# A layer's modulation columns moved from VectorE to ScalarE, and rotary work spread over the units of a weight stream

## The chip, the cores and the metric

One core of a Trainium2 chip. The metric is the device time of one execution in microseconds, median of several runs. Engines are named TensorE (PE in the profile; its weight loads are PEld), VectorE (DVE), ScalarE (ACT), GpSimd (POOL) and the DMA queue of the sync engine (SP).

## What is computed

Two blocks on 256 tokens of width 1024, all in float32. The first block has two layers: a retention layer and a forgetting-attention layer, each modulated by a conditioning vector `c`. The second block is a layer of windowed attention beside a gated recurrence, and a feed-forward network. The part that matters here is the entry of the first layer:

```
shift, scale, gate = jnp.split(c_act @ mod_w[i] + mod_b[i], 3, axis=-1)
h = _rms_norm(x, norm_g[i]) * (1.0 + scale[:, None, :]) + shift[:, None, :]
q, k, v, g = jnp.split(h @ w_in, [RET_DK, 2 * RET_DK, 2 * RET_DK + RET_DV], axis=-1)
q = _rope(q..., positions) * (RET_HK ** -0.5)
k = _rope(k..., positions)
```

`_rope` multiplies halves of each head of 256 by the cosine and sine of position times frequency; the positions are data, so the angles are made in the kernel: a product, a reduction to one turn in several steps, and Sin on ScalarE.

## The kernel before, in words

**Weights as a stream of units.** TensorE multiplies float32 as three products of rounded parts: `whi*ahi + wlo*ahi + whi*alo` (lines 382 to 384, and 493 to 495 in `rows_unit`). All weights pass through one list, `items`. An item "w" is a unit: 128 partitions x 1024 weights (two k-tiles of 512 columns, or one of 1024), 512 KB. SP loads it into one of eight tiles `raw`, ScalarE rounds it to `whi` (line 1796 records all its copies), VectorE subtracts to get `wlo` (line 1057 records all its two-tensor operations), and TensorE uses it for 12 matmuls. There are three buffers of `whi` and `wlo`, so ScalarE makes unit u when TensorE is done with unit u - 3. An item "mod" is a row block of the second layer's modulation weights, or of a gate's: VectorE alone adds it to `acc` (scalar_tensor_tensor, line 1066), in its place in the list. On VectorE and ScalarE `ring_to(u)` does all items up to unit u. Around the change the list reads: mod, 12, mod, 13, mod, 14, mod, 15, mod, 16, 17, 18, mod, 19, 20, 21, mod, 22, 23, 24, 25, mod, 26, 27, 28, mod, 29, 30.

**First layer's h.** Units 0 to 11 are used as the k-tiles of h come. For k-tile k, TensorE sums `c_act @ mod_w` for shift and scale into one column of PSUM each (`own_rows`, line 444, and `other_rows`, line 449, which reads a partial sum `macc` made by VectorE in `mod_sums`) and increments the semaphore `sums`. `modulated(k)` on VectorE makes two columns of `AB` from them: shift plus bias, and (scale + 1 + bias) times the norm's gain, and increments `mod0`. `x0_high(k)` on ScalarE waits for `mod0`, applies the two columns to the transposed normed x (Identity with scale and bias), and rounds to `ahi`; `x0_low(k)` on VectorE makes `alo`. SP waits for `mod0` too, before it loads the fourth and the fifth group of modulation weights (`load_mod`). `mbc` and `mb1` hold bias columns, `g_col` the gains.

**Rotary stage.** Units 12 to 27 are four column chunks of four units: q, q, k, k. A chunk c fills two banks of PSUM, `G[2*(c%2)+m]` for the token halves m = 0, 1. `angles` makes the reduced angles in three parts on VectorE (eleven small operations and a cast), ScalarE takes two Sin of them behind unit 17's `whi`. `rope(n, bank)`, n = 2c + m, is four VectorE operations: two products of 128x512 and two sums of 128x256. TensorE transposes the rope's result (`turn_qk(n)`, line 403): rope 2c - 2 behind the first unit of chunk c, rope 2c - 1 behind the second. Before, VectorE runs all three angle parts ahead of unit 13, and both ropes of a chunk one after the other at the chunk's end. In units 28 to 31 `turn_qk(6)` and `turn_qk(7)` stand behind units 29 and 30, and VectorE's statistics `weighed(0)` behind `ring_to(30)`.

**What sets the order.** Each engine runs its own list, written by hand; VectorE works up to two units ahead of TensorE (`ring_to(u + 2)`). An instruction that waits holds all behind it on its engine. On ScalarE, ahead of unit 14's `whi`, stand the copies of v, a table load and two Silu for the gates. POOL waits for all 32 rope operations before it fills a tile for the second layer's gate.

Of the kernel before, what the change touches and what calls it, by code (L numbers as in the profile page):

```python
# [6 lines left out]
P = 128  # L7
# [10 lines left out]
ALU = mybir.AluOpType  # L18
ACT = mybir.ActivationFunctionType
# [151 lines left out]
def program(nc, x_in, c_in, pos_in, mod_w, mod_b, norm_g, ret_w_in, ret_w_out, fox_w_in, fox_b_f,  # L171
            fox_q_gain, fox_k_gain, fox_w_out, final_g, norm1_w, w_in2, lb_logits, hgrn_nw, w_out2,
            norm2_w, w_gate_up, w_down, final_nw, consts, out):
    with ExitStack() as ctx:
        def sb(name, shape, dt=F32):
            return ctx.enter_context(nc.sbuf_tensor(name, shape, dt))

        sig = Signals(lambda name: ctx.enter_context(nc.semaphore(name)))
# [16 lines left out]
        rows = sb("rows", [P, P])  # L195
        cols = sb("cols", [P, 44])
        mbc = sb("mbc", [P, 16])
        mb1 = sb("mb1", [P, 8])
        cact = sb("cact", [P, 8])
        AB = sb("AB", [P, 2, 16])  # L200
        st = sb("st", [P, 80])
# [16 lines left out]
        G = [ctx.enter_context(nc.psum_tensor(f"G{i}", [P, 512], F32)) for i in range(4)]  # L218
# [10 lines left out]
        g_col = cols[:, 0:16].rearrange("p (a k) -> p a k", a=2)  # L229
# [16 lines left out]
        def sums_of(k, a):  # L246

            return (G[a] if k == 0 else T[a] if k == 1 else T[2 + k % 2])[:, 256 + a:257 + a]
# [801 lines left out]
        def _(e):  # L1050
            on_ = Once(e)

            def bc(ap, *shape):
                return ap.to_broadcast(list(shape))

            def tt(o, a, b, op, name):
                e.tensor_tensor(o, a, b, op).then_inc(sig[name], 1)  # L1057

            def ts(o, a, s1, s2, op0, op1, name):
                if op1 is None:  # L1060
                    e.tensor_scalar(o, a, s1, None, op0).then_inc(sig[name], 1)  # L1061
                else:
                    e.tensor_scalar(o, a, s1, s2, op0, op1).then_inc(sig[name], 1)
# [9 lines left out]
            sums = {}  # L1073
# [24 lines left out]
            def ring_to(u):  # L1098

                while done[0] <= item_of[u]:  # L1100
                    item()
# [24 lines left out]
                    else:  # L1126
                        stt(o, a, col(cact, r), o, ALU.mult, ALU.add, "macc" if last else "mod_sum")

            def modulated(k):

                on_.wait_ge(sig["sums"], k + 1)
                on_.wait_ge(sig["columns"], 3)
                tt(AB[:, 0, 8 + k:9 + k], sums_of(k, 0), mbc[:, k:k + 1], ALU.add, "mod0")
                ts(AB[:, 0, k:k + 1], sums_of(k, 1), mb1[:, k:k + 1], g_col[:, 0, k:k + 1], ALU.add, ALU.mult, "mod0")

            def x0_low(k):
                on_.wait_ge(sig["h_hi"], k + 1)
                tt(alo[:, k, :], stage0[:, k % 4, :], ahi[:, k, :].bitcast(F32), ALU.subtract, "x0")
# [7 lines left out]
            t = T[bank_of["rows"]]  # L1146
            copy(cols[:, 0:44], t[:, 8:52], "columns")
            copy(mbc[:, :], t[:, 54:70], "columns")
            ts(mb1[:, :], t[:, 62:70], 1.0, None, ALU.add, None, "columns")
            modulated(0)  # L1150
            ring_to(0)
            x0_low(0)
            copy(gains[:, 1:2], t[:, 53:54], "rows_read")
            ts(gains[:, 0:1], t[:, 52:53], 0.125, None, ALU.mult, None, "rows_read")
            tt(n1f[:, :], t[:, 70:78], n1_col, ALU.mult, "rows_read")
            mod_sums(1, 0, 4)
            ring_to(1)
            modulated(1)
            ring_to(2)
            x0_low(1)  # L1160
            for g in (2, 3, 4):
                k, u = 2 * g - 2, 3 * g - 3
                mod_sums(g, 0, 4)
                ring_to(u - 1)
                mod_sums(g, 4, 7)
                ring_to(u)
                modulated(k)
                modulated(k + 1)
                x0_low(k)
                ring_to(u + 1)  # L1170
                x0_low(k + 1)
# [19 lines left out]
            def rope(n, src):  # L1191

                m = n % 2
                on_.wait_ge(sig["sincos"], 2)
                on_.wait_ge(sig["rope"], 4 * n)
                A = rot[:, 0, :].rearrange("p (b n) -> p b n", n=P)
                B = rot[:, 1, :].rearrange("p (b n) -> p b n", n=P)
                s = src[:, :].rearrange("p (b n) -> p b n", n=P)
                tt(A, s, bc(cs[:, 0, m, None, :], P, 4, P), ALU.mult, "rope")
                tt(B, s, bc(cs[:, 1, m, None, :], P, 4, P), ALU.mult, "rope")  # L1200
                A4 = rot[:, 0, :].rearrange("p (h t n) -> p h t n", t=2, n=P)
                B4 = rot[:, 1, :].rearrange("p (h t n) -> p h t n", t=2, n=P)
                o = qr[:, n % 2, :].rearrange("p (h t n) -> p h t n", t=2, n=P)
                on_.wait_ge(sig["rope"], 4 * n + 2)
                on_.wait_ge(sig["qk_turned"], n - 1)
                tt(o[:, :, 0, :], A4[:, :, 0, :], B4[:, :, 1, :], ALU.subtract, "rope")
                tt(o[:, :, 1, :], B4[:, :, 0, :], A4[:, :, 1, :], ALU.add, "rope")

            def angles(part):

                BIG, PI = 12582912.0, 3.1415925
                if part == 0:
                    on_.wait_ge(sig["small_in"], 64)
                    copy(posf[:, :], posi[:, :], "posf")
                    on_.wait_ge(sig["small_in"], 64)
                    on_.wait_ge(sig["posf"], 1)
                    for m in range(2):
                        ts(tmp_r[:, m, :], invf, posf[:, m:m + 1], None, ALU.mult, None, "angle")
                    on_.wait_ge(sig["angle"], 2)
                    ts(tmp_k, tmp_r, 1.0 / (2 * np.pi), BIG, ALU.mult, ALU.add, "angle")  # L1220
                    on_.wait_ge(sig["angle"], 3)
                    ts(tmp_k, tmp_k, BIG, None, ALU.subtract, None, "angle")
                elif part == 1:
                    for i, step in enumerate((6.28125, 1014 * 2.0 ** -19, 2 * np.pi - 6.28125 - 1014 * 2.0 ** -19)):
                        on_.wait_ge(sig["angle"], 4 + i)
                        stt(tmp_r, tmp_k, -step, tmp_r, ALU.mult, ALU.add, "angle")
                else:
                    on_.wait_ge(sig["angle"], 7)
                    ts(tmp_k, tmp_r, np.pi / 2, -2 * np.pi, ALU.is_gt, ALU.mult, "angle")
                    on_.wait_ge(sig["angle"], 8)  # L1230
                    stt(tmp_k, tmp_r, np.pi / 2, tmp_k, ALU.add, ALU.add, "angle")
                    on_.wait_ge(sig["angle"], 9)
                    ts(tmp_r, tmp_r, PI, -PI, ALU.min, ALU.max, "angle")
                    ts(tmp_k, tmp_k, PI, -PI, ALU.min, ALU.max, "angle")
# [5 lines left out]

            u = 12
            ring_to(u)
            for part in range(3):
                angles(part)
            for c in range(4):
                for k in range(4):
                    ring_to(u + 2)
                    u += 1
                    if c == 3 and k >= 2:
                        scored(k - 2)  # L1250
                on_.wait_ge(sig["g"], done_at[u - 1, 1])
                for m in range(2):
                    rope(2 * c + m, G[2 * (c % 2) + m])


            def weighed(h):
# [39 lines left out]
            def chunk_of(between):  # L1296
                nonlocal u
                for k in range(4):
                    ring_to(u + 2)
                    u += 1  # L1300
                    for f, *a in between[k]:
                        f(*a)

            chunk_of([[(weighed, 0)], [], [(gated, 0)], [(scored, 2)]])
            chunk_of([[(scored, 3)], [(weighed, 1)], [(left_low, 8)], [(left_low, 10), (gated, 1)]])
            chunk_of([[(weighed, 2)], [(left_low, 12)], [(left_low, 14)], [(gated, 2)]])
            chunk_of([[], [], [(left_low, 16)], [(left_low, 18)]])
# [304 lines left out]
            for k in range(4):  # L1612
# [5 lines left out]
                c, m = k // 2, k % 2  # L1618
# [61 lines left out]
            for m in range(2):  # L1680
                t = T[bank_of["hg_values", m]]
# [107 lines left out]
        def _(e):  # L1789
            on_ = Once(e)  # L1790

            def act(o, a, f, name=None, scale=1.0, bias=0.0, accum=None):
                if accum is not None:
                    d = e.activation(o, a, f, scale=scale, bias=bias, accum_out=accum)
                elif f == ACT.Copy:
                    d = e.activation(o, a, f, scale=scale)  # L1796
                else:
                    d = e.activation(o, a, f, scale=scale, bias=bias)  # L1798
                if name:
                    d.then_inc(sig[name], 1)  # L1800
# [62 lines left out]

            def x0_high(k):

                on_.wait_ge(sig["x0_turned"], k + 1)
                on_.wait_ge(sig["mod0"], 2 * k + 2)
                on_.wait_ge(sig["x0"], k - 3)
                act(stage0[:, k % 4, :], T[2 + k % 2][:, 0:256], ACT.Identity, "h_in", scale=col(AB[:, 0, :], k), bias=col(AB[:, 0, :], 8 + k))
                on_.wait_ge(sig["h_in"], k + 1)  # L1870
                act(ahi[:, k, :], stage0[:, k % 4, :], ACT.Copy, "h_hi")
# [83 lines left out]
            def chunk_of(between):  # L1955
                nonlocal u
                for k in range(4):
                    ring_to(u + 2)
                    u += 1
                    for f, *a in between[k]:  # L1960
                        f(*a)
                on_.wait_ge(sig["g"], done_at[u - 1, 1])
# [187 lines left out]
            for k in range(4):  # L2150
# [3 lines left out]
                c, m = k // 2, k % 2  # L2154
# [255 lines left out]
```

## Time and profile before

| | |
|---|---|
| median of 3 runs | 727.55 us (726.63 to 727.56) |
| profiled execution | 727.51 us, its span 725.7 us |
| TensorE busy | 705.6 us, 97% |
| VectorE busy | 501.6 us, 69% |
| ScalarE busy | 380.0 us, 52% |
| GpSimd busy | 15.9 us, 2% |

Times in the rows are microseconds from the start of the span, and durations of one instruction; instructions of an engine overlap their neighbours by a part of their duration. A bracket at the end of a row is the idle time of the engine ahead of it, and what ended it. Matmul ends are modelled, so starts are the better guide.

### The profile page before, as it was taken

The page shows a single profiled execution, that of the slowest core. Times are in us where ns is not written, and L with a number is a line of the kernel's source. Part 1 is how long each engine was busy: PE and PEld are TensorE (multiplying, and loading weights), DVE is VectorE, ACT ScalarE, POOL GpSimd, SP SyncE. Part 2 cuts the span into 40 slices and gives each one's busy share as a digit, 9 for nine tenths or more (in the row PEclk, how much of TensorE's full clock was granted, in tenths as well). Part 3 has the DMA queues.
Part 4 walks back from the last instruction along what each step waited for, and adds up shares of the span by engine and source line. Part 5 has one row for each costly group of instructions (what it writes and reads, how often), then busy time and mean ns, then how long its engine had stood idle before and what let it go on. Part 6 is the DMA issues. An engine that isn't in the chain of part 4 may idle for free.

```text
span 725.7 us, 9362 instructions
## 1 busy us (share of the span) xinstructions
PE 705.6 (97%) x3534; PEld 577.7 (80%) x3534; DVE 501.6 (69%) x727; ACT 380.0 (52%) x559; POOL 15.9 (2%) x33
## 2 busy tenths in 40 slices
PE   6999999999999999999999899999999999999996
PEld 5887877777887788788887688878888888888884
DVE  4789888787956778665658689955775555555444
ACT  5347544565544565553565654554565445444342
POOL 6000000000000000000000000000000000000000
PEclk8799999999999999999999999999999999999999
DMA  9998865676986357733444553333456655555611
GB/s 295 369 373 312 295 202 182 197 227 210 312 296 205 113 178 249 244 117 115 147 148 143 146 174 117 117 116 117 129 187 206 192 180 180 180 196 178 197 61 58
DMA packets 74476, 138.96 MB, mean 191 GB/s; under 512 B 5748, under 2 KB 18272, under 8 KB 74432
## 3 DMA queue, kind: packets, MB, share of 16 engines
q1 hardware_dynamic: 72816, 134.82, 57.3%
q10 hardware_dynamic: 736, 1.90, 0.7%
q0 software_dynamic: 880, 1.64, 0.6%
q8 instruction: 28, 0.46, 0.3%
q14 instruction: 16, 0.13, 0.1%
HBM read 137.31 MB, written 1.05 MB: 191 GB/s over the span
## 4 chain that ended last, share of the span: by engine, by line
PE 89%; DVE 6%; ACT 2%; issue 2%; DMA 1%; SPq 0%; DVEq 0%; ACTq 0%
PE G L382 23%; PE G L384 23%; PE G L383 22%; PE T L403 5%; PE T L771 2%; DVE wlo L1057 2%; PE T L884 2%; DVE arena L1057 1%; PE T L761 1%; PE G L493 1%; DMA arena<-in_mod_w_dram 1%; PE G L495 1%; PE G L494 1%; PE T L444 1%; ACT whi L1796 1%
## 5 line engine op out<-in xcount | busy, mean ns | idle before, releaser
L1057 DVE TENSOR_TENSOR wlo<-raw,whi 128x1024 fp32r<-128x1024 f32 x202 | 246.1, 1223 | 127.2 <-ACT whi L1796 126.5
L382 PE MATMUL G<-whi,ahi 128*128 128x512 f32 x760 | 307.8, 405 | 4.3 <-DVE wlo L1057 4.3
L384 PE MATMUL G<-whi,alo 128*128 128x512 f32 x760 | 297.0, 391 | 0.0
L383 PE MATMUL G<-wlo,ahi 128*128 128x512 f32 x760 | 296.1, 390 | 0.0
L1796 ACT ACTIVATE whi<-raw 128x1024 fp32r<-128x1024 f32 x202 | 212.9, 1060 | 123.5 <-PE G L384 108.4
L382 PEld LDWEIGHTS G<-whi,ahi 128*128 128x128 f32 x760 | 142.9, 188 | 36.9 <-DVE wlo L1057 8.9
L384 PEld LDWEIGHTS G<-whi,alo 128*128 128x128 f32 x760 | 142.6, 188 | 31.3
L383 PEld LDWEIGHTS G<-wlo,ahi 128*128 128x128 f32 x760 | 143.1, 188 | 28.0 <-issue 1.2
L1798 ACT ACTIVATE arena<-T,st 128x128 f32<-128x128 f32 (+2 forms) x56 | 21.7, 478 | 30.4 <-DVE st L1429 30.4
L1796 ACT ACTIVATE ahi<-T 128x512 fp32r<-128x512 f32 x25 | 15.0, 599 | 41.8 <-PE T L403 41.8
L403 PE MATMUL T<-head,arena 128*128 128x128 f32 x244 | 36.8, 275 | 0.0
L403 PEld LDWEIGHTS T<-head,arena 128*128 128x128 f32 x244 | 29.3, 139 | 9.4 <-issue 2.0
L1798 ACT ACT_TABLE_LOAD x27 | 34.6, 1283 | 2.8 <-issue 1.8
L1066 DVE SCALAR_TENSOR_TENSOR acc<-raw,cact,acc 128x1024 f32<-128x1024 f32 x24 | 30.8, 1282 | 1.1
L1057 DVE TENSOR_TENSOR alo<-T,ahi 128x512 fp32r<-128x512 f32 x25 | 17.3, 691 | 17.7 <-ACT ahi L1796 17.7
L1057 DVE TENSOR_TENSOR arena<-arena 128x512 f32<-128x512 f32 (+7 forms) x46 | 23.0, 551 | 0.8 <-ACT arena L1798 0.5
L1429 DVE TENSOR_REDUCE st<-T 128x2 f32<-128x512 f32 (+1 forms) x18 | 11.6, 686 | 15.5 <-PE T L761 15.5
L1798 ACT ACTIVATE st<-st 128x1 f32<-128x1 f32 (+3 forms) x21 | 4.3, 205 | 26.9 <-DVE st L1061 18.3
L1066 DVE SCALAR_TENSOR_TENSOR arena<-arena,cact 128x512 f32<-128x512 f32 (+1 forms) x24 | 16.4, 685 | 0.8
L884 PEld LDWEIGHTS T<-arena 128*128 128x128 f32 x128 | 15.4, 191 | 0.9 <-DVE arena L1057 0.4
L1796 ACT ACTIVATE arena<-arena 128x512 f32<-128x512 f32 x14 | 8.3, 638 | 14.4 <-DVE arena L1057 14.4
L884 PE MATMUL T<-arena 128*128 128x128 f32 x128 | 15.7, 276 | 0.0
(227 smaller groups left out, 606.8 us busy)
## 6 DMA issues: line engine op xcount, KB each, us to landing
raw<-in_ret_w_in_dram SPq DMA_DIRECT2D x48, 512.0 KB, 5.4
raw<-in_w_gate_up_dram SPq DMA_DIRECT2D x40, 512.0 KB, 3.6
raw<-in_mod_w_dram SPq DMA_DIRECT2D x32, 512.0 KB, 4.8
raw<-in_fox_w_in_dram SPq DMA_DIRECT2D x32, 512.0 KB, 4.8
raw<-in_w_in_dram SPq DMA_DIRECT2D x28, 512.0 KB, 3.5
raw<-in_w_down_dram SPq DMA_DIRECT2D x22, 512.0 KB, 4.3
arena<-in_mod_w_dram SPq DMA_DIRECT2D x16, 512.0 KB, 8.8
raw<-in_ret_w_out_dram SPq DMA_DIRECT2D x16, 512.0 KB, 5.6
```

The lines of the kernel that those rows point to most:

```text
L382: e.matmul(o, ah, wh, start=first and k == 0, stop=False)
L383: e.matmul(o, ah, wl, start=False, stop=False)
L384: done = e.matmul(o, al, wh, start=False, stop=last and k == 1)
L403: d = e.transpose(t[:, n * P:(n + 1) * P], s, idf)
L444: e.matmul(sums_of(SUMMED[g][i], a), mod_tile(g)[:, a, r, i * P:(i + 1) * P], cact[:, r:r + 1], start=r == r0, stop=False)
L771: d = e.matmul(t[:, 65 * a:65 * a + 65], PT[:, g % 2, (a * (m + 1) + j) * P:(a * (m + 1) + j + 1) * P], v[:, j, h, :], start=j == 0, stop= ...
L884: d = e.matmul(t[:, h * P:(h + 1) * P], k[:, h, m * P:(m + 1) * P], q[:, h, m * P:(m + 1) * P], start=True, stop=True)
L1057: e.tensor_tensor(o, a, b, op).then_inc(sig[name], 1)
L1066: e.scalar_tensor_tensor(out=o, in0=a, scalar=s, in1=b, op0=op0, op1=op1).then_inc(sig[name], 1)
L1429: e.tensor_reduce(st[:, 44 + 4 * r:44 + 4 * r + n], t[:, :].rearrange("p (h n) -> p h n", h=n), AX.X, ALU.max, negate=True).then_inc(sig[f ...
L1796: d = e.activation(o, a, f, scale=scale)
L1798: d = e.activation(o, a, f, scale=scale, bias=bias)
```

## The change

It does three things.

1. The first layer's shift and scale columns are made by ScalarE at the head of `x0_high(k)`, as two Identity activations on one column each; `modulated` goes from VectorE. Since (sum + mb1) * g = sum * g + mb1 * g, VectorE makes the product `mb1 * g` for all eight k-tiles once, in a second half of `mb1`.
2. The three parts of `angles` run behind `ring_to(14)`, `ring_to(15)` and `ring_to(16)`, where all three ran behind `ring_to(12)`.
3. Of a chunk's two ropes VectorE does the first at the chunk's end, the second behind the first `ring_to` of the next chunk; rope 7 so moves behind `ring_to(30)`, ahead of `weighed(0)`.

```
-        mb1 = sb("mb1", [P, 8])
+        mb1 = sb("mb1", [P, 2, 8])
...
-            def modulated(k):
-                on_.wait_ge(sig["sums"], k + 1)
-                on_.wait_ge(sig["columns"], 3)
-                tt(AB[:, 0, 8 + k:9 + k], sums_of(k, 0), mbc[:, k:k + 1], ALU.add, "mod0")
-                ts(AB[:, 0, k:k + 1], sums_of(k, 1), mb1[:, k:k + 1], g_col[:, 0, k:k + 1], ALU.add, ALU.mult, "mod0")
...
-            ts(mb1[:, :], t[:, 62:70], 1.0, None, ALU.add, None, "columns")
-            modulated(0)
+            ts(mb1[:, 0, :], t[:, 62:70], 1.0, None, ALU.add, None, "columns")
+            on_.wait_ge(sig["columns"], 3)
+            tt(mb1[:, 1, :], mb1[:, 0, :], g_col[:, 0, :], ALU.mult, "columns")
             ring_to(0)
...
             mod_sums(1, 0, 4)
-            ring_to(1)
-            modulated(1)
             ring_to(2)
...
                 ring_to(u)
-                modulated(k)
-                modulated(k + 1)
                 x0_low(k)
...
             ring_to(u)
-            for part in range(3):
-                angles(part)
             for c in range(4):
                 for k in range(4):
                     ring_to(u + 2)
                     u += 1
-                    if c == 3 and k >= 2:
+                    if c == 0 and k < 3:
+                        angles(k)
+                    elif c and k == 0:
+                        rope(2 * c - 1, G[2 * ((c - 1) % 2) + 1])
+                    elif c == 3 and k >= 2:
                         scored(k - 2)
                 on_.wait_ge(sig["g"], done_at[u - 1, 1])
-                for m in range(2):
-                    rope(2 * c + m, G[2 * (c % 2) + m])
+                rope(2 * c, G[2 * (c % 2)])
...
-            chunk_of([[(weighed, 0)], [], [(gated, 0)], [(scored, 2)]])
+            chunk_of([[(rope, 7, G[3]), (weighed, 0)], [], [(gated, 0)], [(scored, 2)]])
...
             def x0_high(k):
+                on_.wait_ge(sig["columns"], 4)
+                on_.wait_ge(sig["sums"], k + 1)
+                act(AB[:, 0, 8 + k:9 + k], sums_of(k, 0), ACT.Identity, "mod0", bias=mbc[:, k:k + 1])
+                act(AB[:, 0, k:k + 1], sums_of(k, 1), ACT.Identity, "mod0", scale=g_col[:, 0, k:k + 1], bias=mb1[:, 1, k:k + 1])
                 on_.wait_ge(sig["x0_turned"], k + 1)
                 on_.wait_ge(sig["mod0"], 2 * k + 2)
```

## Rows read from the trace of the kernel before

**Rows 1.** The page's busy times: us, share of the span, instructions.
```profile
PE 705.6 (97%) x3534; PEld 577.7 (80%) x3534; DVE 501.6 (69%) x727; ACT 380.0 (52%) x559; POOL 15.9 (2%) x33
```

**Rows 2.** Waits over 0 to 150 us: us in total, times, longest.
```profile
PE G L382 <- DVE wlo L1057: 1.3, 3, 0.7
```

**Rows 3.** Timeline of TensorE over 0 to 42: start, us, engine, line, what.
```profile
15.07 0.76 PE L493 MATMUL G<-whi,ahi 128*128 128x512 f32 x1 [0.72 <-DVE alo L1057]
...
40.54 0.36 PE L449 MATMUL T<-ones,arena 128*128 128x1 f32 x2
```

**Rows 4.** Timeline of TensorE over 62 to 94.
```profile
64.85 0.39 PE L384 MATMUL G<-whi,alo 128*128 128x512 f32 x1
65.98 0.50 PE L382 MATMUL G<-whi,ahi 128*128 128x512 f32 x1 [0.74 <-DVE wlo L1057]
...
77.19 0.66 PE L403 MATMUL T<-head,arena 128*128 128x128 f32 x4
77.60 0.48 PE L382 MATMUL G<-whi,ahi 128*128 128x512 f32 x1
...
92.26 0.60 PE L403 MATMUL T<-head,arena 128*128 128x128 f32 x4
93.13 0.50 PE L382 MATMUL G<-whi,ahi 128*128 128x512 f32 x1 [0.28 <-DVE wlo L1057]
```

**Rows 5.** Timeline of VectorE over 59 to 93.
```profile
59.48 0.16 DVE L1069 CAST posf<-posi 128x2 f32<-128x2 int32 x1
...
62.23 0.37 DVE L1063 TENSOR_SCALAR arena<-arena 128x256 f32<-128x256 f32 x1
...
63.51 1.28 DVE L1066 SCALAR_TENSOR_TENSOR acc<-raw,cact,acc 128x1024 f32<-128x1024 f32 x1
64.71 1.22 DVE L1057 TENSOR_TENSOR wlo<-raw,whi 128x1024 fp32r<-128x1024 f32 x1
...
72.29 2.35 DVE L1057 TENSOR_TENSOR wlo<-raw,whi 128x1024 fp32r<-128x1024 f32 x2
75.05 1.29 DVE L1057 TENSOR_TENSOR arena<-G,gate 128x512 f32<-128x512 f32 x2 [0.41 <-ACT gate L1798]
...
86.55 1.29 DVE L1057 TENSOR_TENSOR arena<-G,gate 128x512 f32<-128x512 f32 x2 [0.27 <-PE G L384]
...
88.66 1.29 DVE L1057 TENSOR_TENSOR arena<-G,gate 128x512 f32<-128x512 f32 x2
...
91.86 2.35 DVE L1057 TENSOR_TENSOR wlo<-raw,whi 128x1024 fp32r<-128x1024 f32 x2
```

**Rows 6.** Timeline of ScalarE over 64 to 75.
```profile
64.21 2.18 ACT L1796 ACTIVATE whi<-raw 128x1024 fp32r<-128x1024 f32 x2
69.13 1.06 ACT L1796 ACTIVATE whi<-raw 128x1024 fp32r<-128x1024 f32 x1 [2.74 <-PE G L384]
...
71.85 1.06 ACT L1796 ACTIVATE whi<-raw 128x1024 fp32r<-128x1024 f32 x1
...
74.23 0.72 ACT L1798 ACTIVATE gate<-arena 128x256 f32<-128x256 f32 x2
```

**Rows 7.** Timeline of VectorE over 13 to 41.
```profile
13.01 0.16 DVE L1057 TENSOR_TENSOR AB<-G,mbc 128x1 f32<-128x1 f32 x1 [0.52 <-PE G L449]
13.08 0.27 DVE L1063 TENSOR_SCALAR AB<-G,mb,cols 128x1 f32<-128x1 f32 x1
...
38.14 2.32 DVE L1066 SCALAR_TENSOR_TENSOR arena<-arena,cact 128x512 f32<-128x512 f32 x3
```

**Rows 8.** Timeline of ScalarE over 8 to 15.
```profile
8.91 0.20 ACT L1798 ACTIVATE st<-st 128x2 f32<-128x2 f32 x1
...
13.45 0.56 ACT L1798 ACTIVATE gate<-T,AB 128x256 f32<-128x256 f32 x1 [1.27 <-DVE AB L1063]
14.05 0.42 ACT L1796 ACTIVATE ahi<-gate 128x256 fp32r<-128x256 f32 x1
```

**Rows 9.** Stretch of 20 us: length, TensorE busy, granted clock, DMA share, GB/s.
```profile
20.00:40.00 20.00, 20.00 (x93) 0.84 1.07 369
```

## The prediction, made before the result was known

> **What bounds the kernel now.** I read the page first: TensorE is busy for 97% of the span [rows 1]. So a part of the change counts only where it makes TensorE wait longer or shorter. The list of waits over the first 150 us says where that can be: 1.3 us in three waits for `wlo` [rows 2]; the timeline of TensorE adds one of 0.72 for the first `alo` [rows 3].
>
> The timelines show what each wait costs. The first matmul on weights starts at 15.07, behind `alo` of k-tile 0 [rows 3]. Unit 12's last matmul starts at 64.85, and with the usual spacing of 0.23 unit 13 could start at 65.08; it starts at 65.98: 0.90 lost [rows 4]. ScalarE's `whi` of unit 16 follows the end of unit 13, and comes 3.15 behind 65.98, where a unit without a wait takes 2.72 (69.13 to 71.85) and the hand-over 0.26: another 0.17 in slower matmuls behind the wait [rows 6]. The first transposes of a rope start at 77.19, about 0.15 later than TensorE could. Unit 22 waits until 93.13, where 92.26 + 0.4 would do (a unit starts 0.4 behind its transposes, 77.19 and 77.60): 0.47; the same stands at 105.49 in the next column chunk [rows 4]. In sum 1.07 + 0.15 + 0.47 + 0.47 = 2.2 us that could be had, all of it waits for VectorE.
>
> VectorE has no pause from 59.48 to 74.64: angles, then mod and `wlo` in turn; the first rope starts at 75.05 [rows 5]. The order of its work against ScalarE's decides.
>
> **Part 1, columns on ScalarE.** Removed from VectorE: eight pairs of 0.34 us (13.01 to 13.35 for the first) [rows 7]. Added: the same eight pairs on ScalarE, and one product of 8 columns on VectorE, which by the one-column row takes some 0.16 and is over before 13.01. A ScalarE instruction on two columns takes 0.20. The one on 128x256 with two pointer operands takes 0.56, the copy without 0.42, so a pointer costs about 0.07 [rows 8]. The pair has one and two pointers: 0.27 + 0.34, less some 0.08 by which neighbours overlap: 0.53. Bounds: 0.3 (as on VectorE) and 0.65 (no overlap). I take 0.53, since the rows price just these operands. The hand-over between engines, 0.10 (13.35 to 13.45), becomes a wait of the engine on itself, 0.04 (14.05 less the end of the one before it, 14.01). So h of k-tile 0 starts at 13.01 + 0.53 + 0.04 = 13.58 instead of 13.45 [rows 8], and the first matmul 0.13 later.
>
> The Trainium skill (ScalarE: Activation LUTs, What ACT_TABLE_LOAD costs) gives 280 ns to a one-column ACTIVATE with one pointer operand, 93 ns more for each further one, and 93 ns of overlap. By it the pair would take 0.56 and the start come 0.16 later instead of 0.13; it speaks against moving one-column operations to this engine.
>
> For k-tiles 2, 4 and 6 the same 0.13 meets matmuls that have about as much room. For 3, 5 and 7 the pair stands behind the split of the k-tile before it, so h and the next `whi` come up to 0.5 later, and VectorE's sums for the next group start up to 0.15 later. The last of these ends at 40.46, and the matmul that reads it starts at 40.54 [rows 7, 3]: I add 0.1. SP's two mod loads that wait for `mod0` go out 0.2 to 0.5 later; the DMA share is 1.07 in this stretch [rows 9], so they would queue behind others anyway and cost nothing; without that cover they would cost 0.5. **Part 1: +0.2** (bounds -0.1 and +0.5).
>
> **Part 2, angles.** Costs on VectorE, start to start: `wlo` 1.13 (half of 2.35 with its overlap), mod 1.20 (63.51 to 64.71), angle parts 0 and 1 together 2.75, part 2 1.28; parts 0 and 1 are about 0.1 less each when the next instruction doesn't depend on them, so 1.28 too [rows 5]. The work ahead of the first rope is the same before and after. What changes is what VectorE does while ScalarE is late: ScalarE has a table load and two Silu ahead of unit 14's `whi`, which starts at 64.21 [rows 6]. Before, the angles filled this time. After, VectorE has mod, `wlo` 13 and mod done by 63.6 and then waits: `whi` 14 ends at 64.21 + 1.06, `wlo` 14 starts at 65.37. Unit 13 starts at 65.08 without a wait, so TensorE is 1.07 ahead. But then VectorE does:
> - `wlo` 14 at 65.37, angles 0 66.50, mod 67.78, `wlo` 15 68.98 to 70.20. Unit 15 wants it at 65.08 + 2 x 2.72 = 70.52: no wait.
> - angles 1 70.11, mod 71.39, `wlo` 16 72.59 to 73.81. Unit 16 wants it at 73.24 and starts at 73.87: 0.63 of the gain is gone, and 0.17 in slower matmuls.
> - angles 2 73.72, `wlo` 17 75.00, rope 0 at 76.13. The pair of Sin (0.72 [rows 6], its table loaded before) starts at about 75.1 and ends at 75.8: no further wait.
>
> Before, rope 0 started at 75.05, so it is 1.08 later. Its transposes come 2.14 behind its start (75.05 to 77.19 [rows 5, 4]), at 78.27; TensorE is free for them at 76.8 and waits 1.5 us. Behind them the distances stay. **Part 2: +1.08**, the gain at unit 13 already in it. Bounds: 0, if ScalarE makes `whi` 14 a microsecond sooner than before; +1.4, if the angle parts don't shrink.
>
> **Part 3, ropes of the second halves.** A rope takes 2.11 to the next rope and 2.00 to other work (88.66 to 91.86, less a mod) [rows 5]. Chunk 1: rope 0 76.13, `wlo` 18 78.13, rope 1 79.26, its transposes possible at 81.40; TensorE comes to them at 78.27 + 0.41 + 2.8 = 81.5 (0.41 from transposes to unit, and a unit a little over its 2.72). No wait, and no gain, as unit 18 did not wait before. Chunk 2, in times of before: rope 2 starts at 86.55, then comes a mod, which stands ahead of unit 22 in the stream, then `wlo` 22, then rope 3 at 86.55 + 2.00 + 1.20 + 1.13 = 90.88, transposes at 93.02. TensorE wants them at 92.26. Unit 22 follows at 93.43, where it started at 93.13 [rows 4, 5]. A wait of 0.8 ahead of the transposes takes the place of the one for `wlo` 22: +0.30. Chunk 3 has the same order, with a mod ahead of unit 26: +0.30. In the chunk behind, rope 7 trades places with `wlo` 30 ahead of the first statistics, and its transposes are two units off: 0. The banks that the second ropes free are wanted a chunk later, and POOL's fill behind all ropes, 1 us later, has a whole layer of room. **Part 3: +0.6** (bounds +0.3 and +0.9).
>
> **Sum.** 0.2 + 1.08 + 0.6 = +1.9. Nothing behind gives it back: TensorE sets the pace and loads are issued as units are used. The profiled execution took 727.51 for its span of 725.7, and the median is 727.55, the same: 729.4. What this kernel's measurement can tell from no change is about 0.2%, 1.45 us.
>
> **Rivals.**
> 1. The waits simply go: `wlo` 13, 22 and 26 are in time and no rope is missed. Price -1.07 - 0.47 - 0.47 + 0.1: 725.6. For it: each is a wait for a `wlo`, and each `wlo` moves forward. Against it: rope 0 would have to start by 75.05 and rope 3 0.8 sooner than its durations add up to. It decides if VectorE finds `whi` 14 ready at 63.6. If only that holds and part 3 doesn't change, it is 727.5 - 1.2 + 0.6 + 0.2 = 727.1. Faster by over 0.2%: 0.13.
> 2. A wash: VectorE packs closer than I add up, so that rope 0 is late by half of 1.08 and one of the chunks loses nothing: +1.0, 728.5. For it: terms of 0.1 decide. Within 0.2%, with the half case above: 0.27.
> 3. The wait of 1.5 us lets TensorE's clock fall. Behind the wait of 0.74 at 65.98 a unit takes 2.72 as ever [rows 4, 6]; over 20 to 40 the mean granted clock was 0.84, so some 6 us stood at the lower of its two levels (1.2 GHz of 2.4) [rows 9]. The same again costs 3 us more: 732.5. Chance 0.04, inside slower.
>
> My forecast holds slower by over 0.2% at 0.60. The range for 8 in 10 goes from 727.0 (the wash and the half case are in) to 731.0 (all upper bounds but the clock).
>
> **What would show it.** Right: VectorE idle for some 1.8 us ahead of `wlo` 14, for ScalarE; no wait of TensorE at unit 13, one of some 0.6 at unit 16, one of 1.5 ahead of the transposes behind it, 0.8 ahead of the transposes behind units 21 and 25, none at units 22 and 26; the first weight matmul at about 15.2, ScalarE's pair at 0.5. Wrong: a rope 0 that starts by 75.1, a pair of 0.3, or the transposes behind unit 21 without a wait.

## The result, and the profile after

The changed kernel takes 730.15 us (median of 18 runs, 728.21 to 733.42); the kernel before, run beside it, 728.64 (18 runs, 725.6 to 730.02). The ratio is 1.0032, with a 95% interval of 1.0021 to 1.0044: **slower by 2.3 us** (1.5 to 3.2). The prediction was +1.9.

The page of the changed kernel's profile, busy times (us, share, instructions), answers to [rows 1]:

```profile
PE 703.0 (97%) x3534; PEld 575.1 (79%) x3534; DVE 498.5 (69%) x712; ACT 383.6 (53%) x575; POOL 16.6 (2%) x33
```

VectorE has 15 instructions less and ScalarE 16 more, as eight pairs and one product should give. But TensorE was busy 2.6 us less while the kernel became slower, and the profiled span is 726.2, only 0.5 longer. That comes from the start, where TensorE's clock stands at its lower level for a while. Two stretches of before, then of after (length, busy time of PE, PEld, DVE, ACT, POOL, granted clock, DMA share, GB/s):

```profile
12.00:20.00 8.00, 7.28 (x33) 6.33 (x31) 5.41 (x15) 4.50 (x7) 0.51 (x2) 0.54 1.10 337
20.00:26.00 6.00, 6.00 (x20) 5.13 (x21) 3.82 (x8) 1.60 (x3) 0.00 (x0) 0.50 1.07 376
```

```profile
12.00:20.00 8.00, 7.06 (x34) 6.11 (x33) 5.84 (x16) 5.40 (x9) 0.37 (x1) 0.57 1.10 337
20.00:26.00 6.00, 5.25 (x29) 4.24 (x29) 3.69 (x6) 1.74 (x5) 0.00 (x0) 1.00 1.07 375
```

Over 20 to 26 the clock is 0.50 before (1.2 of 2.4 GHz) and 1.00 after. The same differs between profiles of one and the same early code. Over 20 to 22 TensorE, busy throughout, did 10 or 11 matmuls in seven of the ten profiles of this study and 15 or 16 in three, with either form of the columns on both sides. The first column instruction starts anywhere from 12.9 to 15.5. So whole spans don't compare here, nor do times from the span's start; I compare distances between fixed instructions.

**The distances.** I take four stages, each from one profile of each kernel: (a) from the first column instruction to the first matmul on weights; (b) from k-tile 2's sum (its first matmul of line 449, at 30.09 before and 28.72 after; by then the slow start is over in all ten profiles) to unit 12; (c) from unit 12 to unit 28; (d) from unit 28 to the end. The stretch between (a) and (b), in which k-tile 1 is made, is in none of them, because the slow start lies in it; what part 1 costs there is looked at below. The rows that bound (c), before, then after:

```profile
62.35 0.39 PE L382 MATMUL G<-whi,ahi 128*128 128x512 f32 x1
...
113.64 0.47 PE L382 MATMUL G<-whi,ahi 128*128 128x512 f32 x1
```

```profile
61.30 0.39 PE L382 MATMUL G<-whi,ahi 128*128 128x512 f32 x1
...
114.06 0.48 PE L382 MATMUL G<-whi,ahi 128*128 128x512 f32 x1
```

Stage (c) takes 51.29 before and 52.76 after: +1.47. Unit 12 itself came 1.05 sooner, and that is the start, not the change: stage (b) is 0.32 longer (28.72 to 61.30 is 32.58, before 30.09 to 62.35 is 32.26), stage (a) 0.16 longer, stage (d) 612.14 for 612.06. The sum is 1.95, inside the interval of the runs.

The list of waits over 61 to 114 (us in total, times, longest) names (c)'s; before, the only line of TensorE was that of [rows 2]:

```profile
PE T L403 <- DVE arena L1057: 2.5, 3, 1.3
PE G L382 <- DVE wlo L1057: 0.4, 1, 0.4
```

Three waits for ropes and one for a `wlo` stand where three waits for a `wlo` were. TensorE's timeline places them (start, us, what), against [rows 3, 4]:

```profile
15.95 0.76 PE L493 MATMUL G<-whi,ahi 128*128 128x512 f32 x1 [0.94 <-DVE alo L1057]
...
72.77 0.50 PE L382 MATMUL G<-whi,ahi 128*128 128x512 f32 x1 [0.43 <-DVE wlo L1057]
...
77.09 0.66 PE L403 MATMUL T<-head,arena 128*128 128x128 f32 x4 [1.31 <-DVE arena L1057]
77.50 0.48 PE L382 MATMUL G<-whi,ahi 128*128 128x512 f32 x1
...
92.92 0.66 PE L403 MATMUL T<-head,arena 128*128 128x128 f32 x4 [0.60 <-DVE arena L1057]
93.33 0.47 PE L382 MATMUL G<-whi,ahi 128*128 128x512 f32 x1
...
105.55 0.66 PE L403 MATMUL T<-head,arena 128*128 128x128 f32 x4 [0.60 <-DVE arena L1057]
```

Unit 13 waits no more; unit 16 waits 0.43, the first rope's transposes 1.31, the transposes behind units 21 and 25 0.60 each, and units 22 and 26 not at all. VectorE's timeline, against [rows 5], has the cause:

```profile
64.32 1.23 DVE L1057 TENSOR_TENSOR wlo<-raw,whi 128x1024 fp32r<-128x1024 f32 x1 [1.65 <-ACT whi L1787]
65.46 0.16 DVE L1069 CAST posf<-posi 128x2 f32<-128x2 int32 x1
...
67.91 1.22 DVE L1057 TENSOR_TENSOR wlo<-raw,whi 128x1024 fp32r<-128x1024 f32 x1
...
71.50 1.22 DVE L1057 TENSOR_TENSOR wlo<-raw,whi 128x1024 fp32r<-128x1024 f32 x1
...
74.96 1.28 DVE L1057 TENSOR_TENSOR arena<-G,gate 128x512 f32<-128x512 f32 x2
...
88.46 1.28 DVE L1066 SCALAR_TENSOR_TENSOR acc<-raw,cact,acc 128x1024 f32<-128x1024 f32 x1
89.65 1.22 DVE L1057 TENSOR_TENSOR wlo<-raw,whi 128x1024 fp32r<-128x1024 f32 x1
90.79 1.28 DVE L1057 TENSOR_TENSOR arena<-G,gate 128x512 f32<-128x512 f32 x2
```

VectorE is idle for 1.65 ahead of `wlo` 14, and has all of the angles still to do. Rope 0 starts at 74.96, 13.66 behind unit 12 where it was 12.70. In chunk 2 (last three rows) a mod and `wlo` 22 stand between the two ropes. ScalarE's pair, against VectorE's of [rows 7] and h of [rows 8]:

```profile
13.73 0.26 ACT L1789 ACTIVATE AB<-G,mbc 128x1 f32<-128x1 f32 x1 [1.16 <-PE G L449]
13.89 0.35 ACT L1789 ACTIVATE AB<-G,mb,cols 128x1 f32<-128x1 f32 x1
14.33 0.56 ACT L1789 ACTIVATE gate<-T,AB 128x256 f32<-128x256 f32 x1
```

### The profile page after: what moved, and what is told of

The parts are those of the page before. It is cut to its first block, busy times and chain, and to the rows that moved or that the text cites. A ratio compares the mean times of both kernels' runs of the same rounds, so it can differ in the third digit from the quotient of the medians.

```text
span 726.2 us, 9366 instructions
## 1 busy us (share of the span) xinstructions
PE 703.0 (97%) x3534; PEld 575.1 (79%) x3534; DVE 498.5 (69%) x712; ACT 383.6 (53%) x575; POOL 16.6 (2%) x33
## 3 DMA queue, kind: packets, MB, share of 16 engines
HBM read 137.31 MB, written 1.05 MB: 191 GB/s over the span
## 4 chain that ended last, share of the span: by engine, by line
PE 86%; DVE 7%; ACT 3%; issue 2%; DMA 1%; SPq 0%; DVEq 0%; ACTq 0%
PE G L382 23%; PE G L384 22%; PE G L383 22%; PE T L403 5%; PE T L771 2%; DVE wlo L1057 2%; PE T L884 2%; DVE arena L1057 2%; PE T L761 1%; DMA arena<-in_mod_w_dram 1%; PE G L493 1%; PE G L495 1%; PE G L494 1%; ACT whi L1787 1%; DVE arena L1066 1%
## 5 line engine op out<-in xcount | busy, mean ns | idle before, releaser
L1787 ACT ACTIVATE arena<-T 128x512 f32<-128x512 f32 x11 | 6.5, 598 | 19.2 <-PE T L403 16.4
```

## The experiments

Eight kernels ran besides, none leaving out a part of the computation: ratios are to the kernel before, run on the same chip between them. Two of the rivals were ruled out by the profile of after: the waits did not simply go, and no clock fell behind the wait of 1.31 (over 77 to 83 the granted clock is 1.00). What the runs had to tell was which part costs what, whether an idle VectorE is really the cause, and what a pair of columns costs. All the results together, in us; (a), (b) and (c) as differences to before, (d) whole:

| kernel | (a) | (b) | (c) | (d) | a + b + c | ratio [95%] | by the ratio |
|---|---|---|---|---|---|---|---|
| changed kernel | 0.16 | 0.32 | 1.47 | 612.14 | 1.95 | 1.0032 [1.0021, 1.0044] | 2.3 |
| columns_only | 0.15 | 0.33 | 0.23 | 612.11 | 0.71 | 1.0008 [0.9994, 1.0022] | 0.6 |
| angles_only | 0 | 0 | 0.99 | 611.95 | 0.99 | 1.0012 [0.9998, 1.0026] | 0.9 |
| ropes_only | 0 | 0.17 | 0.55 | 611.96 | 0.72 | 1.0001 [0.9989, 1.0014] | 0.1 |
| angles_in_gap | 0.16 | 0.28 | 0.44 | 612.06 | 0.88 | 1.0013 [1.0000, 1.0026] | 0.9 |
| ropes_mods_off | 0.01 | 0.03 | -1.12 | 612.06 | -1.08 | 0.9982 [0.9971, 0.9993] | -1.3 |
| mods_only | 0.01 | 0.02 | -1.09 | 611.93 | -1.06 | 0.9985 [0.9971, 0.9999] | -1.1 |
| columns_twice | 0.56 | 2.89 | 0.62 | 612.14 | 4.07 | 1.0058 [1.0038, 1.0078] | 4.2 |
| best | 0 | 0 | -2.13 | 612.01 | -2.13 | 0.9964 [0.9950, 0.9978] | -2.6 |

Each sum lies in the interval of its runs, and (d) is the same within 0.2 throughout, so nothing is given back or lost behind unit 28. The intervals of columns_only, angles_only and ropes_only hold 1, so the price of each part by itself rests on the distances alone. The 0.17 of ropes_only in (b), ahead of every edit of it, shows what (b) is good for: about 0.2. It goes with the fast start, which ropes_only shares with columns_only and the changed kernel. Like with like, the pair costs in (b) 0.16 (columns_only less ropes_only) or, with the slow start, 0.28 (angles_in_gap less before). The stretch between (a) and (b) is 12.59 in columns_only and 12.46 in ropes_only, and 14.98 in angles_in_gap and 15.02 before. With (a), part 1 so costs about 0.4 by either comparison. The sum of columns_twice holds a fall of the clock as well (see there).

**columns_only**: part 1 alone, as in the change (`modulated` gone from VectorE); angles and ropes as before.

```
...
 def x0_high(k):
+    on_.wait_ge(sig["columns"], 4)
+    on_.wait_ge(sig["sums"], k + 1)
+    act(AB[:, 0, 8 + k:9 + k], sums_of(k, 0), ACT.Identity, "mod0", bias=mbc[:, k:k + 1])
+    act(AB[:, 0, k:k + 1], sums_of(k, 1), ACT.Identity, "mod0", scale=g_col[:, 0, k:k + 1], bias=mb1[:, 1, k:k + 1])
```

> The kernel before with part 1 alone: ScalarE makes the columns. Theory (each part costs what its own stage shows, and they add): the span from VectorE's or ScalarE's first one-column instruction to the first weight matmul is 2.22 us, 0.16 longer than before (2.06), and the stage from unit 12 to unit 28 stays at 51.3 us, as before, with the three waits for wlo in it; time 0 to +0.4 us. Rival (the columns give the gain that their stage seems to show in the changed kernel, where unit 12 starts 1.05 us sooner): unit 12 starts about 61.3 here too, and the time falls by 1 us. Second rival (that start is the luck of TensorE's clock): unit 12's start follows how long the matmuls behind 15 us keep the spacing of 0.43, whatever the kernel.

Measured 729.18 (12 runs) against 727.98 for before (35 runs). The runs alone can't tell this from no change, but the stages do: 0.71, of which 0.23 lies at unit 13, where no part-1 work is left. Its timeline of TensorE:

```profile
64.92 0.50 PE L382 MATMUL G<-whi,ahi 128*128 128x512 f32 x1 [0.96 <-DVE wlo L1057]
```

The wait was 0.74 [rows 4]. VectorE came late out of the stage before, since a `wlo` there waits for a `whi` that ScalarE makes later; its timeline:

```profile
54.73 1.23 DVE L1057 TENSOR_TENSOR wlo<-raw,whi 128x1024 fp32r<-128x1024 f32 x1 [0.59 <-ACT whi L1786]
```

Against unit 12 this `wlo` comes 0.46 later than before (6.34 ahead of it for 6.80), and a part of that reaches `wlo` 12 and the angles: the cast that begins the angles starts 2.65 ahead of unit 12 (58.42 to 61.07), where it was 2.87 (59.48 [rows 5] to 62.35). In the full change this lateness should cost nothing, since VectorE waits for `whi` 14 there anyway; that rope 0 starts equally far behind unit 12 with and without part 1 (13.66, see angles_only) agrees.

**angles_only**: part 2 alone.

```
-            for part in range(3):
-                angles(part)
...
+                    if c == 0 and k < 3:
+                        angles(k)
```

> The kernel before with part 2 alone: an angle part behind each of ring_to(14), (15), (16), both ropes still at a chunk's end. Theory (VectorE idles ahead of wlo 14 and pays with the angles later): idle of 1.6 us ahead of wlo 14, no wait of TensorE at unit 13, one of 0.4 at unit 16, one of 1.3 ahead of the first transposes; unit 12 to unit 28 is 52.2 us, 0.9 longer than before (51.3); the waits of 0.28 ahead of units 22 and 26 stay. Time +0.9. Rival (the angles are harmless and the ropes carry the whole loss): 50.2 to 51.3 us, time -1 to 0.

Measured 729.4, (c) longer by 0.99. The waits are those of the changed kernel, unit 16's and the first rope's, and that of unit 22 is back as in [rows 4]; its timeline of TensorE:

```profile
75.84 0.50 PE L382 MATMUL G<-whi,ahi 128*128 128x512 f32 x1 [0.43 <-DVE wlo L1057]
...
80.16 0.66 PE L403 MATMUL T<-head,arena 128*128 128x128 f32 x4 [1.28 <-DVE arena L1057]
...
96.12 0.50 PE L382 MATMUL G<-whi,ahi 128*128 128x512 f32 x1 [0.28 <-DVE wlo L1057]
```

Rope 0 starts 13.66 behind unit 12, to the hundredth as in the changed kernel.

**ropes_only**: part 3 alone.

```
-                for m in range(2):
-                    rope(2 * c + m, G[2 * (c % 2) + m])
+                rope(2 * c, G[2 * (c % 2)])
...
+                    if c and k == 0:
+                        rope(2 * c - 1, G[2 * ((c - 1) % 2) + 1])
...
```

> The kernel before with part 3 alone: the second rope of a chunk one unit later, behind a mod and a wlo. Theory: the wait at unit 13 stays (0.74), the first transposes stay at about 14.8 us behind unit 12, two waits of 0.6 (idle) ahead of the transposes behind units 21 and 25 take the place of those ahead of units 22 and 26; unit 12 to unit 28 is 51.9 us, 0.6 longer. Time +0.6. Rival (the ropes are neutral or gain, VectorE gets the wlo out first): 50.8 to 51.3 us, time -0.5 to 0.

Measured 728.33, (c) longer by 0.55. Unit 13 waits as before, and the transposes behind unit 21 wait; its timeline of TensorE:

```profile
66.03 0.50 PE L382 MATMUL G<-whi,ahi 128*128 128x512 f32 x1 [0.75 <-DVE wlo L1057]
...
93.05 0.66 PE L403 MATMUL T<-head,arena 128*128 128x128 f32 x4 [0.59 <-DVE arena L1057]
```

Parts 2 and 3 alone add up to 0.99 + 0.55 = 1.54; together they cost 1.47. They don't share a wait.

**angles_in_gap**: the changed kernel with one edit. If VectorE's idle time ahead of `wlo` 14 is the cause, filling it with an angle part must bring rope 0 forward.

```
-            ring_to(u)
+            ring_to(u + 1)
+            angles(0)
...
-                    if c == 0 and k < 3:
-                        angles(k)
+                    if c == 0 and k in (0, 2):
+                        angles(1 + k // 2)
```

> The changed kernel with the first angle part behind ring_to(13), so in the time in which VectorE waits for ScalarE's whi of unit 14, and the others behind ring_to(14) and ring_to(16). Theory (the idle time ahead of wlo 14 is what the change lost): that idle time falls from 1.65 to about 0.3, no wait at unit 16, the first rope starts 1.2 us sooner against unit 12 than in the changed kernel; unit 12 to unit 28 falls from 52.8 to 51.6 us; time 1.2 below the changed kernel, still some 0.5 above the kernel before, for the ropes and the columns. Rival (the angle parts themselves are dearer among units, or SP's loads are what is late): 52.4 us or more.

Measured 729.11, (c) 51.73, 1.03 less than in the changed kernel. VectorE's timeline, the gap and rope 0:

```profile
65.64 1.23 DVE L1057 TENSOR_TENSOR wlo<-raw,whi 128x1024 fp32r<-128x1024 f32 x1 [0.52 <-ACT whi L1788]
...
75.22 1.28 DVE L1057 TENSOR_TENSOR arena<-G,gate 128x512 f32<-128x512 f32 x2
```

The gap shrinks from 1.65 to 0.52, by 1.13 (0.3 was expected to be left). Unit 12 starts at 62.61 here, so rope 0 comes 12.61 behind it instead of 13.66: 1.05 sooner. What went into the gap comes off the stage. The three waits for transposes that are left (2.2 us in sum, the longest 1.0) hold the rest: part 3's two, and rope 0's, since TensorE now arrives without its stop at unit 13.

**ropes_mods_off**: ropes_only with the second layer's mods that stood ahead of units 22 and 26 put behind units 23 and 27. It tests whether that mod, which stands between the two ropes, is what makes the second one late.

```
-    after = (-1, 0, 1, 2, 3, 6, 9, 13, 16, ...
+    after = (-1, 0, 1, 2, 3, 6, 11, 15, 16, ...
```

**mods_only**: the kernel before, with the five mods behind units 14, 15, 18, 21 and 25 put behind units 18, 19, 23, 24 and 27, and nothing else: is it the ropes' place or the mods' place that pays?

```
-    after = (-1, 0, 1, 2, 3, 6, 9, 13, 16, ...
+    after = (-1, 0, 1, 6, 7, 11, 12, 15, 16, ...
```

> ropes_only with the mod ahead of unit 22 put behind unit 23 and the one ahead of unit 26 behind unit 27. Theory (a mod and a wlo between two ropes is what made the second rope late): VectorE reaches the end of rope 3 at about 91.8 in times of before, ahead of TensorE's 92.26, so neither the transposes behind unit 21 and 25 nor units 22 and 26 wait; only the wait at unit 13 (0.74) is left; unit 12 to unit 28 is 50.4 us, 0.9 below the kernel before and 1.5 below ropes_only. Time -0.9. Rival (the second rope is late because TensorE's transposes and ScalarE's copies queue up behind it, or its wlo is late anyway): waits of 0.3 or more stay in both chunks and the stage is 51 us or more.

> The kernel before with nothing but the mods moved as in best; angles and ropes as before. Theory: the wait at unit 13 stays (0.74), those ahead of units 22 and 26 go, as wlo 22 and 26 stand right behind the ropes; the stage is 50.4 us; time -0.9. Against best this tells what the new places of angles and ropes add (1.1 us, all at unit 13). Rival (moving the mods only moves the wait, to units 19 to 21 or 24): a new wait of 0.3 or more between units 19 and 28.

Measured 726.75 and 726.86 (before beside them 727.9, 26 runs), (c) 50.17 and 50.20: 1.1 below before both. The list of waits of mods_only over 62 to 115 has one line, unit 13's (the other kernel has the same one, 0.7):

```profile
PE G L382 <- DVE wlo L1057: 0.8, 1, 0.8
```

So with the mods out of the way the ropes' place is worth nothing either way: 0.03 lies between the two kernels. The two don't move the same mods, but in both only the wait at unit 13 is left, so the three that mods_only moves besides have nothing more to win. Without moving any, part 3 costs 0.55.

**columns_twice**: columns_only with the pair made twice, the first time into the unused half of `AB`. Doubling the pair prices it, and shows how much room the groups behind have.

```
+    act(AB[:, 1, 8 + k:9 + k], sums_of(k, 0), ACT.Identity, "mod0_again", bias=mbc[:, k:k + 1])
+    act(AB[:, 1, k:k + 1], sums_of(k, 1), ACT.Identity, "mod0_again", scale=g_col[:, 0, k:k + 1], bias=mb1[:, 1, k:k + 1])
```

> columns_only with each pair made twice on ScalarE (the first time into columns that nobody reads then), so part 1's added work doubled. Theory (the pair sits on the chain to the first matmul and delays ScalarE behind each odd k-tile): the first weight matmul comes 2.65 us behind the first column instruction (2.21 with one pair, 2.06 before), VectorE is later behind unit 11, and the wait at unit 13 grows from 0.96 to 1.2 or more; the stage from unit 12 to 28 is 51.7 to 51.9. Rival (ScalarE has room there and the 0.2 at unit 13 is chance): 2.65 at the start, but the wait at unit 13 stays at 0.74 to 0.96.

Measured 732.27 (6 runs). (a) is 2.62, 0.41 more than with one pair (2.21), and (c) 51.91, with a longer wait at unit 13. But (b) is 35.15, 2.6 more than with one pair, and that was not foreseen. Two things lie in it. One is the waits; its timeline of TensorE, then of VectorE:

```profile
34.75 0.47 PE L493 MATMUL G<-whi,ahi 128*128 128x512 f32 x1 [0.26 <-DVE alo L1057]
...
42.69 0.38 PE L449 MATMUL T<-ones,arena 128*128 128x1 f32 x2 [0.27 <-DVE arena L1066]
...
70.73 0.50 PE L382 MATMUL G<-whi,ahi 128*128 128x512 f32 x1 [1.40 <-DVE wlo L1057]
```

```profile
34.18 0.42 DVE L1057 TENSOR_TENSOR alo<-gate,ahi 128x256 fp32r<-128x256 f32 x1 [2.46 <-ACT ahi L1786]
...
36.08 0.42 DVE L1057 TENSOR_TENSOR alo<-gate,ahi 128x256 fp32r<-128x256 f32 x1 [0.34 <-ACT ahi L1786]
...
40.31 2.32 DVE L1066 SCALAR_TENSOR_TENSOR arena<-arena,cact 128x512 f32<-128x512 f32 x3
```

TensorE waits for the first `alo` in two of the three groups of two k-tiles (34.75, and 0.25 at 58.21) and once for the partial sum of the next group (42.69). ScalarE has h, `ahi`, two pairs and two `whi` on one path there, and VectorE's sums stand behind the second `alo`.

The other is the clock, which falls to its lower level once more, inside (b). Two stretches (as above):

```profile
44.00:46.00 2.00, 2.00 (x9) 1.67 (x9) 0.11 (x1) 1.58 (x7) 0.00 (x0) 0.66 1.02 400
46.00:48.00 2.00, 2.00 (x7) 1.42 (x6) 1.68 (x3) 1.89 (x7) 0.00 (x0) 0.50 1.06 405
```

From 44.58 to 48.23 nine steps from matmul to matmul take 3.65, where at 0.23 they would take 2.1: some 1.6 us. Ahead of the fall TensorE had waited 0.27 (42.69) and then done its one-column sums, which stand there in the other kernels too, without a fall. By groups, against one pair: 11.39 for 10.63 (+0.76), 12.07 for 10.61 (+1.46, the one with the fall) and 11.69 for 11.35 (+0.34). So the second pair costs at least 1.1 in the two groups at full clock, and what it alone would have cost in the middle one stays open. The room in a group that the prediction counted on nearly covers one pair and doesn't cover a second.

**best**: the kernel before with part 3, the first angle part in the gap and the other two behind units 14 and 15's work, and the mods moved as in mods_only. The columns stay on VectorE.

```
+            ring_to(u + 1)
+            angles(0)
...
+                    if c == 0 and k < 2:
+                        angles(1 + k)
...
-    after = (-1, 0, 1, 2, 3, 6, 9, 13, 16, ...
+    after = (-1, 0, 1, 6, 7, 11, 12, 15, 16, ...
```

> Parts 2 and 3 without part 1, the first angle part behind ring_to(13), the others behind ring_to(14) and (15), and the mods ahead of units 15, 16, 19, 22 and 26 moved to places behind units 18 to 27 where VectorE has idle time. Theory (VectorE's work between units 13 and 17 is the sum that counts, and two mods of 1.2 us each out of it let rope 0 start when the Sin are there): no wait of TensorE over 0.2 us from unit 12 to unit 28, rope 0 starts 11.6 us behind unit 12 (12.7 before), the stage is 49.3 us, 2.0 below before; time -2.0. Rival (ScalarE is next: whi or Sin come late by as much): the wait at unit 13 goes, but one of 0.7 or more comes ahead of the first transposes and the stage is 50 us or more.

Measured 725.55 (9 runs), 0.9964 [0.9950, 0.9978]: it beats the kernel before by 2.6 us (1.6 to 3.6) and the changed kernel by more. No wait of TensorE is left between unit 12 and unit 28, and (c) is 49.16. VectorE's timeline:

```profile
65.55 1.23 DVE L1057 TENSOR_TENSOR wlo<-raw,whi 128x1024 fp32r<-128x1024 f32 x1 [0.63 <-ACT whi L1799]
...
74.15 1.29 DVE L1057 TENSOR_TENSOR arena<-G,gate 128x512 f32<-128x512 f32 x2 [0.81 <-ACT gate L1801]
```

Rope 0 starts 11.62 behind unit 12 (62.53), and what ends its wait is now ScalarE's Sin, not VectorE's own work.

## Why the prediction was right

**Part 2** held link by link. Behind unit 12 (62.35 in the working, 61.30 in the trace of after): `wlo` 14 was put at 3.02 and came at 3.02; `wlo` 15 at 6.63, came at 6.61; `wlo` 16 at 10.24, came at 10.20; rope 0 at 13.78, came at 13.66; its transposes at 15.92, came at 15.79. VectorE's idle time was put at 1.8 and was 1.65: the mod ahead of it ended 1.37 behind unit 12 (64.32 less 1.65), where the working had 1.25 (63.6 less 62.35). The 63.6 doesn't follow from the working's own prices: 59.48 + 1.20 + 1.13 + 1.20 is 63.0, with an idle time of over 2. In the trace of after a mod starts 1.32 behind the `wlo` ahead of it (57.53 to 58.85, 60.06 to 61.38), not 1.13. Nothing else rested on it, since `wlo` 14 waits for ScalarE in either case. The term was +1.08; rope 0 is 0.96 later and angles_only costs 0.99. That the gap is the cause is shown by angles_in_gap, where 1.13 less of idle time brought 1.05.

**Part 3**: +0.6 predicted, +0.55 alone. The distance from rope 2's start to the transposes of rope 3 was put at 93.02 - 86.55 = 6.47, and is 92.92 - 86.46 = 6.46. The waits were to be 0.8 and are 0.60; unit 22's start behind rope 2's is 6.87 (93.33 - 86.46) for 6.58 before, +0.29. The lever was the mod between the ropes: ropes_mods_off takes 1.7 off (c) (51.84 to 50.17) by moving two mods.

**Part 1** is the term that was mis-sized. The pair was put at 0.53 and takes 0.51 (13.73 to 13.89 + 0.35), h starts 0.60 behind it (0.57 was predicted) where it was 0.44, and the first matmul comes 0.16 later, not 0.13. By the figures of the Trainium skill (ScalarE: Activation LUTs, What ACT_TABLE_LOAD costs) the pair would take 0.56, an estimate that is 0.05 too high here. What the prediction drew from them, that such operations are better not moved to this engine, held. What failed is the 0.1 for the groups behind: (b) is 0.32 longer. The prediction had the second k-tile's h late by up to 0.5 and the sums behind it by 0.15, and took that as paid once. In the first group of after that h starts 2.96 behind k-tile 2's sum (31.68), before 2.21 (32.30), so 0.75 later. The trace shows it in the first group behind (b)'s start:

```profile
28.72 0.38 PE L449 MATMUL T<-ones,arena 128*128 128x1 f32 x2 [0.16 <-DVE arena L1066]
```

```profile
32.73 0.42 DVE L1057 TENSOR_TENSOR alo<-gate,ahi 128x256 fp32r<-128x256 f32 x1
...
36.97 2.32 DVE L1066 SCALAR_TENSOR_TENSOR arena<-arena,cact 128x512 f32<-128x512 f32 x3
```

The last partial sum starts 8.25 behind the group's first matmul (36.97 - 28.72), before it was 38.14 - 30.09 = 8.05 [rows 7]: 0.2 later, and the group takes 10.63 for 10.45. The sum of three groups is 0.3. So part 1 costs 0.16 + 0.32 = 0.48 by these stages, or about 0.4 between kernels with the same start: twice the 0.2, near its upper bound of 0.5. With 0.48 the terms make 0.48 + 0.96 + 0.55 = 2.0, and the runs say 2.3 (1.5 to 3.2). That SP's loads cost nothing was not tried by itself; the DMA share over 20 to 22 is 1.09 in both kernels.

**The rivals.** The waits did not simply go (1): it needed `whi` 14 to be there when VectorE was, and VectorE waited 1.65 for it. Its price was sound all the same: best, which has no wait, gains 2.13 in (c), and the prediction had found 2.2 to be had. The wash (2) asked for rope 0 to be late by half of 1.08; it was late by 0.96. The clock (3) stayed at 1.00 behind the long wait, in the one execution that was profiled. In columns_twice it fell behind a wait of 0.27, so that a wait's length doesn't tell by itself whether it falls.

## What to carry to other kernels

An engine's filler work is worth where it stands, not what it costs: before spreading it, find the idle time that it fills (here VectorE's, ahead of `wlo` 14), since work moved out of a gap is paid in full later. When two pieces are moved apart, look at what then falls between them (here a mod, which could be moved instead, for a gain of 1.1). And where the effect is 0.3% and the runs of one kernel spread over 0.6%, distances between fixed instructions tell parts apart that the times can't, if the clock was the same on both sides of the comparison.

## What had not been expected of the hardware

The slow stretch at the start is not a property of the kernel. Over 20 to 22, with TensorE busy throughout, it did 10 or 11 matmuls in before, best, ropes_mods_off, mods_only, angles_only, angles_in_gap and columns_twice, and 15 or 16 in the changed kernel, columns_only and ropes_only. In the unit behind k-tile 1's sum the matmuls of lines 493 to 495 start 0.43 us apart in the first seven and 0.23 apart in the other three.

The granted clock of the profile doesn't always tell. In angles_only and ropes_only it reads 1.00 from 12 us on, yet the matmuls of these lines start 0.43 apart up to 27.70 in angles_only and up to 19.78 in ropes_only. The stretch of 20 to 22 of before, angles_only and ropes_only:

```profile
20.00:22.00 2.00, 2.00 (x11) 2.00 (x11) 0.00 (x0) 0.00 (x0) 0.00 (x0) 0.50 1.09 347
20.00:22.00 2.00, 2.00 (x11) 1.98 (x10) 0.34 (x1) 0.00 (x0) 0.00 (x0) 1.00 1.09 349
20.00:22.00 2.00, 2.00 (x16) 1.90 (x15) 0.53 (x1) 0.02 (x1) 0.00 (x0) 1.00 1.10 350
```

The first two have 11 matmuls each, at a clock recorded as 0.50 and as 1.00; the third has 16. So the spacing of equal matmuls is the surer sign, and a 1.00 near the start of a trace wants checking against it.

Unit 12 came no sooner in ropes_only (62.40, before 62.35), although its slow stretch ended earlier, as the first column instruction came at 15.45 instead of 13.01. What sets that start, and when the clock falls, stays open.
